# Prologue of a hybrid decoder layer on TensorE: spreading the norm row by products of high and low halves, other counts of idle turns, and the first weight's high half ahead of all token copies on ScalarE

## The chip, the cores and the metric

The kernel runs on one core of a Trainium2 chip. The metric is the device time of one execution in microseconds (us). A core has TensorE (PE; its weight loads are listed apart as PEld), VectorE (DVE), ScalarE (ACT), GpSimd (POOL) and SyncE (SP), which here only issues transfers. The engines run their own instruction lists in order and wait for each other by semaphores.

## The reference, cut to what matters

One inference step of a decoder layer with 512 prompt tokens and 32 sample tokens of width 1024. The first thing that it computes is a root-mean-square norm with a weight row `g`, and a large projection of the result; attention, a recurrent branch and a feed-forward block follow.

```python
def rmsnorm(x, g):
    x32 = x.astype(jnp.float32)
    y = x32 * lax.rsqrt(jnp.mean(x32 * x32, axis=-1, keepdims=True) + RMS_EPS)
    return (y * g.astype(jnp.float32)).astype(x.dtype)
...
    h = rmsnorm(x, g_mix_pre)
    proj = h @ w_in
```

## The kernel before

Every large product is made from high and low halves. A tile of fp32 numbers is rounded to the matmul type fp32r (the high half, a Copy on ScalarE), the rest is the fp32 number less its high half (the low half, a subtraction on VectorE or GpSimd), and TensorE adds three products: high by high, high by low, low by high. The activations `xin_hi`, `xin_lo` lie with the model dimension on the partitions, 8 tiles of 544 tokens; weights pass through a ring of two slots, `w_raw`, `w_hi`, `w_lo`.

The change touches only the prologue, that is what happens before the loop over heads. There, for five groups of tokens (four of 128, `tt` = 0 to 3, and one of 32, `tt` = TT):

- SyncE loads `x_tok` of groups 0 and 1, then weight tile 0 (`w_raw[0]`, in two transfers), groups 2 and 3, weight tile 1, and the sample tokens, in this order.
- `x_rms(tt)` on ScalarE squares and sums a group (L1684) and takes a root (L1687). `hi(0, 0, 0)` rounds weight tile 0 (L1662), and `x_hi` copies transposed tokens from PSUM to `xin_hi` (L1696), by halves of 512 columns for groups 0 to 3.
- The norm's row stands in partition 127 of `g_one`, whose other 127 partitions VectorE clears. A product with a tile of ones (`g_rows`, L1116) spreads it over 128 partitions in PSUM, and `g_copy` (L2261) on VectorE brings it to `g_row`, in two halves. `x_inv` is the reciprocal (L2266), `x_scale` the scaling of the tokens by it and by `g_row` (L2271), and `x_lo` the subtraction that leaves `xin_lo` (L2283).
- TensorE transposes scaled tokens (`x_T`, L1106), computes a small bias table (L1126, L1127), and then runs the first passes of the projection with weight tiles 0 and 1 over the columns of groups 0 and 1 (`head_pass`, L1288): three for each tile, of 8 products each. `turn(n)` is n transposes of the identity whose result nobody reads (L1113).
- GpSimd clears some tiles and makes the low half of weight tile 0 (L946) once `w_hi[0]` is there.

The order of all this is written out by hand, engine by engine. Where an instruction waits, the rest of its engine's list waits behind it. The first projection pass needs both the rounded weight and three halves of tokens, as the lines on TensorE have it:

```python
            e.wait_ge(hi_done, 1)
            e.wait_ge(xt_hi, 3)
            head_pass(0, 0, w_hi[0], xin_hi, first=True, k1=KD // 2)
            e.wait_ge(xt_hi, 4)
            head_pass(0, 0, w_hi[0], xin_hi, first=True, k0=KD // 2)
```

Of the kernel before, what the change touches and what calls it, by code (L numbers as in the profile page):

```python
# [23 lines left out]
F32 = mybir.dt.float32  # L24
F32R = mybir.dt.float32r
I32 = mybir.dt.int32
ALU = mybir.AluOpType
ACT = mybir.ActivationFunctionType
AP = bass.AP

P = 128
D = 1024
KD = D // P
# [3 lines left out]
T = SEQ + TS  # L37
# [74 lines left out]
X_ORDER = (0, 1, 2, 3, TT)  # L112
# [18 lines left out]
def program(nc, x_prompt, x_sample, cache_k, cache_v, page_table, state_conv, state_h,  # L131
# [11 lines left out]
    at = [-(-nc.sbuf_base // 64) * 64]  # L143

    def put(name, shape, dt=F32, where=None):
        size = 4 * int(np.prod(shape[1:]))
        size = -(-size // 32) * 32
        if where is None:
            offset, at[0] = at[0], at[0] + size
        else:  # L150
            offset, where[0] = where[0], where[0] + size
        assert offset + size <= nc.sbuf_usable_end, (name, offset + size)
        return nc.alloc_sbuf_tensor_at(name, shape, dt, offset=offset)
# [3 lines left out]
    w_raw, w_hi, w_lo = ring  # L157
    xin_at = at[0]
    xin_hi = put("xin_hi", [P, KD, T], F32R)
    xin_lo = put("xin_lo", [P, KD, T], F32R)  # L160
    ident = put("ident", [P, P])
    ones = put("ones", [P, P])
# [58 lines left out]
    x_sq = put("x_sq", [P, D], where=w)  # L221
    g_row = put("g_row", [P, D], where=w)
    g_one = put("g_one", [P, D], where=w)
    ssum = put("ssum", [P, 8], where=w)
    rstd_x = put("rstd_x", [P, 8], where=w)
    prow = put("prow", [56, P], where=w)
# [157 lines left out]
    with ExitStack() as ctx:  # L384
        def sem(name):
            return ctx.enter_context(nc.semaphore(name))

        ps = ctx.enter_context(nc.psum_tensor("ps", [P, 8, 512], F32))
# [12 lines left out]
        g_in = sem("g_in")  # L401
        g_spread = sem("g_spread")
# [4 lines left out]
        consts_v = sem("consts_v")  # L407
        sq_sum = sem("sq_sum")
        std_x = sem("std_x")
        norm_step = sem("norm_step")  # L410
# [661 lines left out]
        def _(e):  # L1072
# [21 lines left out]
            def x_T(tt, hfs=None):  # L1094

                rows = P if tt < TT else TS
                for hf in range(2 if tt < TT else 1) if hfs is None else hfs:
                    f = X_HALF[tt] + hf
                    e.wait_ge(xs_done, 2 * tt + hf + 1 if tt < 2 else X_ORDER.index(tt) + 3)
                    if tt == TT:  # L1100
                        e.wait_ge(sp_act, 2)
                    elif f >= 4:
                        e.wait_ge(xt_lo, f - 3)
                    kts = range(4 * hf, 4 * hf + 4) if tt < TT else range(KD)
                    for n, kt in enumerate(kts):
                        mm = e.transpose(ps[:, 4 + f % 4 if tt < TT else 3, n * rows:(n + 1) * rows],  # L1106
                                         x_tok[0:rows, tt, kt * P:kt * P + P], ident[0:rows, 0:rows])
                    mm.then_inc(xt_ready, 1)

            def turn(n):  # L1110

                for _ in range(n):
                    e.transpose(ps[:, 0, 0:P], ident[:, :], ident[:, :])  # L1113

            def g_rows(hf):
                e.matmul(ps[:, 1 + hf, :], ones[:, :], g_one[:, 512 * hf:512 * hf + 512], start=True, stop=True  # L1116
                         ).then_inc(g_spread, 1)

            turn(7)
            e.wait_ge(consts_v, 6)  # L1120
            e.wait_ge(g_in, 16)
            g_rows(0)
            g_rows(1)
            e.wait_ge(norm_step, 1)
            e.wait_ge(rel_in, 32)
            e.matmul(ps[:, 3, 0:512], rel33[:, :], bktab[:, 0:512], start=True, stop=True)  # L1126
            e.matmul(ps[:, 1, 0:RELW - 512], rel33[:, :], bktab[:, 512:RELW], start=True,  # L1127
                     stop=True).then_inc(small_T, 1)
            x_T(0, (0,))
            turn(5)  # L1130
            x_T(0, (1,))
            turn(4)
            x_T(1)
            turn(2)

# [521 lines left out]
        def _(e):  # L1657
# [18 lines left out]
            e.dma_start(rel33[0:NB, 0:HEADS], rel_bias).then_inc(rel_in, 16)  # L1676
            e.wait_ge(consts_v, 5)
            e.activation(ycol[:, 0:1], eps_col[:, :], ACT.Sqrt)

            def x_rms(tt):  # L1680

                rows = P if tt < TT else TS
                e.wait_ge(x_in[tt], 16)
                e.activation(x_sq[0:rows, :], x_tok[0:rows, tt, :], ACT.Square,  # L1684
                             accum_out=ssum[0:rows, tt:tt + 1]).then_inc(sq_sum, 1)
                e.wait_ge(sq_sum, X_ORDER.index(tt) + 1)
                e.activation(rstd_x[0:rows, tt:tt + 1], ssum[0:rows, tt:tt + 1], ACT.Sqrt,  # L1687
                             bias=eps_col[0:rows, :], scale=1.0 / D).then_inc(std_x, 1)

            def x_hi(tt, hfs=None):  # L1690

                for hf in range(2 if tt < TT else 1) if hfs is None else hfs:
                    f = X_HALF[tt] + hf
                    e.wait_ge(xt_ready, f + 1)
                    dst, src = x_fill(xin_hi, tt, hf, f)
                    e.activation(dst, src, ACT.Copy).then_inc(xt_hi, 1)  # L1696

            x_rms(0); x_rms(1)
            x_hi(0, (0,))
            hi(0, 0, 0)  # L1700
            x_hi(0, (1,))
            x_hi(1)
            x_rms(2)
            e.wait_ge(small_T, 1)
# [523 lines left out]
        def _(e):  # L2228
# [30 lines left out]
            def g_copy(hf):  # L2259
                e.wait_ge(g_spread, hf + 1)  # L2260
                e.tensor_copy(g_row[:, 512 * hf:512 * hf + 512], ps[:, 1 + hf, :]).then_inc(norm_step, 1)  # L2261

            def x_inv(tt):
                rows = slice(0, P if tt < TT else TS)
                e.wait_ge(std_x, X_ORDER.index(tt) + 1)
                e.reciprocal(rstd_x[rows, tt:tt + 1], rstd_x[rows, tt:tt + 1]).then_inc(norm_step, 1)  # L2266

            def x_scale(tt, step, c0=0, c1=D):
                rows = slice(0, P if tt < TT else TS)
                e.wait_ge(norm_step, step)  # L2270
                e.scalar_tensor_tensor(x_tok[rows, tt, c0:c1], x_tok[rows, tt, c0:c1], rstd_x[rows, tt:tt + 1],  # L2271
                                       g_row[rows, c0:c1], ALU.mult, ALU.mult).then_inc(xs_done, 1)

            def x_norm(tt):
                x_inv(tt)
                x_scale(tt, X_ORDER.index(tt) + 3)

            def x_lo(tt):
                for hf in range(2 if tt < TT else 1):
                    f = X_HALF[tt] + hf  # L2280
                    e.wait_ge(xt_hi, f + 1)
                    dst, src = x_fill(xin_lo, tt, hf, f)
                    e.tensor_tensor(dst, src, x_fill(xin_hi, tt, hf, f)[0].bitcast(F32), ALU.subtract).then_inc(xt_lo, 1)  # L2283

            g_copy(0)
            x_inv(0)
            x_scale(0, 2, 0, 512)
            g_copy(1)
            x_scale(0, 3, 512, D)
            x_inv(1)  # L2290
            x_scale(1, 4, 0, 512)
            x_scale(1, 4, 512, D)
            x_lo(0)
            x_lo(1)
            x_norm(2)
# [529 lines left out]
            op_sums(0)  # L2825
            op_low(0, 5)
            e.memset(yacc[:, :], 0.0).then_inc(consts_v, 1)
            e.wait_ge(consts_v, 7)
            y_square(0, 0)
            op_low(0, 6)  # L2830
            hs_low(2, 3)
# [75 lines left out]
```

## Time and profile before

| | |
|---|---|
| median of 3 runs | 761.62 us (760.98 to 761.72) |
| the profiled execution | 761.57 us, of which the span of its instructions is 759.7 us |
| TensorE busy | 751.6 us, 99% of the span |
| VectorE, ScalarE, GpSimd busy | 519.8, 376.5, 116.4 us |
| chain that ended last | 99% TensorE |
| TensorE's granted clock, mean | 0.997 |

The span is the time from the first to the last instruction that the profiler recorded. The busy shares are averages over the whole; the prologue is the first 20 us or so, and it has to be read by itself, in the order of time. Ends of TensorE's products are modelled, so the starts are the better measure of its pace.

### The profile page before, as it was taken

Reading aid. Unit: us, or ns where it says so; the run is one execution under the profiler, and the core shown is the slowest. Engines: PE = TensorE matmul, PEld = TensorE weight load, DVE = VectorE, ACT = ScalarE, POOL = GpSimd, SP = SyncE. Lnnn points to the kernel's source line nnn. Section 1 sums busy time; section 2 is a strip of 40 time slices with the busy share of each in tenths; the row PEclk is TensorE's granted clock in tenths of the full one; section 3 lists DMA queues with packets and bytes.
Section 4 is the critical chain, followed back from the end, with each engine's and each line's share of the span. In section 5 each row is a group of like instructions: output and inputs, shape, how many; then the busy total and the mean of one; then the engine's idle time right before and its main releaser. Section 6 shows DMA issues by size and latency. Waiting matters only on the chain.

```text
span 759.7 us, 16105 instructions
## 1 busy us (share of the span) xinstructions
PE 751.6 (99%) x5903; PEld 713.0 (94%) x5903; DVE 519.8 (68%) x823; ACT 376.5 (50%) x670; POOL 116.4 (15%) x228
## 2 busy tenths in 40 slices
PE   9999999999999999999999999999999999999996
PEld 6998899898898999997899999999999999999996
DVE  7547737656675574775469887787777899764644
ACT  7334625534733642344466555455554568454442
POOL 6502112020120110003000000000000000453650
PEclk9999999999999999999999999999999999999998
DMA  9645555545543325517461333223332212424274
GB/s 265 164 112 118 151 118 135 149 113 109 153 115 97 95 65 171 167 56 212 147 190 34 112 110 110 85 81 110 110 110 83 84 50 73 137 75 133 69 227 135
DMA packets 185065, 91.77 MB, mean 121 GB/s; under 512 B 52454, under 2 KB 177850, under 8 KB 185020
## 3 DMA queue, kind: packets, MB, share of 16 engines
q1 hardware_dynamic: 178958, 82.69, 39.8%
q0 software_dynamic: 4880, 8.13, 4.0%
q8 instruction: 28, 0.46, 0.3%
q10 hardware_dynamic: 1182, 0.35, 0.2%
q14 instruction: 17, 0.14, 0.1%
HBM read 82.37 MB, written 6.81 MB: 117 GB/s over the span
## 4 chain that ended last, share of the span: by engine, by line
PE 99%; ACT 0%; DVE 0%; DVEq 0%; issue 0%; POOL 0%; POOLq 0%
PE ps L1082 34%; PE ps L1470 28%; PE ps L1587 7%; PE ps L1365 6%; PE ps L1572 5%; PE ps L1534 4%; PE ps L1438 3%; PE ps L1288 2%; PE ps L1189 1%; PE ps L1203 1%; PE ps L1221 1%; PE ps L1263 1%; PE ps L1174 1%; PE ps L1234 1%; PE ps L1116 0%; PE ps L1373 0%
## 5 line engine op out<-in xcount | busy, mean ns | idle before, releaser
L1082 PE MATMUL ps<-xin_hi,w_hi 128*128 128x272 f32 x544 | 117.1, 296 | 0.0
L1082 PE MATMUL ps<-xin_hi,w_lo 128*128 128x272 f32 x544 | 112.6, 288 | 0.0
L1082 PE MATMUL ps<-xin_lo,w_hi 128*128 128x272 f32 x544 | 112.3, 288 | 0.0
L1082 PEld LDWEIGHTS ps<-xin_hi,w_hi 128*128 128x128 f32 x544 | 84.8, 189 | 8.1 <-issue 7.6
L2248 DVE TENSOR_TENSOR w_lo<-w_raw,w_hi 128x1024 fp32r<-128x1024 f32 (+1 forms) x46 | 55.9, 1216 | 47.6 <-ACT w_hi L1662 46.6
L1082 PEld LDWEIGHTS ps<-xin_lo,w_hi 128*128 128x128 f32 x544 | 85.5, 189 | 0.0
L1082 PEld LDWEIGHTS ps<-xin_hi,w_lo 128*128 128x128 f32 x544 | 85.0, 189 | 0.0
L648 POOL DMA_DIRECT2D ytok<-yz x48 | 33.8, 710 | 307.9 <-DVE yz L2809 307.9
L1662 ACT ACTIVATE w_hi<-w_raw 128x1024 fp32r<-128x1024 f32 (+1 forms) x47 | 49.2, 1050 | 47.9 <-PE ps L1082 44.0
L1470 PE MATMUL ps<-xq_lo,b_hi 128*128 128x272 f32 x160 | 46.7, 292 | 0.0
L1470 PE MATMUL ps<-xq_hi,a_lo 128*128 128x272 f32 x160 | 46.4, 290 | 0.0
L1470 PE MATMUL ps<-xq_lo,a_hi 128*128 128x272 f32 x160 | 46.2, 289 | 0.0
L1470 PE MATMUL ps<-xq_hi,b_hi 128*128 128x272 f32 x160 | 46.2, 289 | 0.0
L1470 PE MATMUL ps<-xq_hi,b_lo 128*128 128x272 f32 x160 | 46.1, 288 | 0.0
L1470 PE MATMUL ps<-xq_hi,a_hi 128*128 128x272 f32 x160 | 46.1, 288 | 0.0
L1470 PE MATMUL ps<-xq_hi,c_hi 128*128 128x272 f32 x160 | 46.1, 288 | 0.0
L1470 PE MATMUL ps<-xq_hi,c_lo 128*128 128x272 f32 x160 | 45.9, 287 | 0.0
L1470 PE MATMUL ps<-xq_lo,c_hi 128*128 128x272 f32 x160 | 45.9, 287 | 0.0
L1985 ACT ACTIVATE a_hi<-g_raw 128x1024 fp32r<-128x1024 f32 x20 | 21.2, 1062 | 21.1 <-PE ps L1470 17.9
L1470 PEld LDWEIGHTS ps<-xq_hi,b_hi 128*128 128x128 f32 x160 | 30.2, 189 | 0.0
L1470 PEld LDWEIGHTS ps<-xq_hi,b_lo 128*128 128x128 f32 x160 | 30.1, 188 | 0.0
L1470 PEld LDWEIGHTS ps<-xq_lo,a_hi 128*128 128x128 f32 x160 | 30.1, 188 | 0.0
(397 smaller groups left out, 2136.6 us busy)
## 6 DMA issues: line engine op xcount, KB each, us to landing
w_raw<-in_w_in_dram SPq DMA_DIRECT2D x68, 256.0 KB, 3.5
g_raw<-in_w_gate_up_dram SPq DMA_DIRECT2D x40, 256.0 KB, 3.8
u_raw<-in_w_gate_up_dram SPq DMA_DIRECT2D x20, 256.0 KB, 3.1
e_raw<-in_w_gate_up_dram SPq DMA_DIRECT2D x20, 256.0 KB, 4.3
raw_p<-in_w_down_dram SPq DMA_DIRECT2D x24, 192.0 KB, 2.5
kc<-in_cache_k_dram SPq DMA_DIRECT2D x64, 64.0 KB
vc<-in_cache_v_dram SPq DMA_DIRECT2D x64, 64.0 KB
raw<-in_w_down_dram SPq DMA_DIRECT2D x12, 320.0 KB, 3.2
```

Source lines behind the costliest of these rows:

```text
L648: e.dma_start(prompt[:, 2 * part:2 * part + 2, d, :], yz[s][rows, c0:c0 + 2 * P]).then_inc(moved, 16)
L1082: mm = e.matmul(ps[:, bank + h, 0:HT], wt[:, kw, :], xt[:, kx, h * HT:h * HT + HT], start=first and wt is wh and xt is xh, stop=last and ( ...
L1288: mm = e.matmul(ps[:, 2 * s + h, 0:cols.stop - cols.start], w[:, k, :], x[:, k, cols], start=first and k == 0, stop=last and k == KD - 1, ...
L1365: mm = e.matmul(ps[:, o_bank(tt) + c, :], xt[:, k, tt * P:tt * P + P], wt[:, c * NHALF:(c + 1) * NHALF], start=k == K_ORDER[0] and xt is x ...
L1438: mm = e.matmul(ps[:, 4 * m + 2 * c + h, 0:HT], wt[:, k, :], xt[:, x, k % KQ, :], start=k == 0 and wt is wh and xt is xq_hi, stop=k == KD ...
L1470: mm = e.matmul(ps[:, bank, 0:HT], wt[:, k0 + k, :], xt[:, x, k, :], start=first and k == 0 and wt is wh and xt is xq_hi, stop=last and k ...
L1534: mm = e.matmul(ps[:, D_BANK[odd] + h, 0:cols.stop - cols.start], wt[:, k, :], x, start=first and k == ks[0] and wt is wh and not lo_x, st ...
L1572: mm = e.matmul(ps[:, bank, 0:HT], wt[:, k, :], xt, start=first and k == 0 and wt is wh and xt is xh, stop=last and k == SK - 1 and wt is ...
L1587: mm = e.matmul(ps[:, banks[h], 0:HT], wt[:, k, :], x, start=firsts[h] and i == 0 and k == 0 and wt is wh and not lo_x, stop=lasts[h] and ...
L1662: e.activation((to or w_hi[s])[:, 0:k, :], w_raw[s][:, 0:k, :], ACT.Copy).then_inc(hi_done, count)
L1985: e.activation(a_hi[:, :, :], g_raw[s][:, :, :], ACT.Copy).then_inc(a_h, 1)
L2248: e.tensor_tensor(wl[:, 0:k, :], w_raw[s][:, 0:k, :], wh[:, 0:k, :].bitcast(F32), ALU.subtract).then_inc(lo_done, count)
```

## The change

It has three parts. The row `g` is split into a high half (`g_hi`, first 512 columns on VectorE, last 512 on ScalarE) and a low half (`g_lo`, both by VectorE), and is spread by two fp32r products per half with a tile of ones in fp32r (`ones_r`) in place of one fp32 product. On VectorE, both `g_copy` now stand ahead of the first reciprocal. The idle turns are 11, 2, 3 and 2 instead of 7, 5, 4 and 2. On ScalarE, `hi(0, 0, 0)` goes ahead of the first half of the tokens of group 0, where it stood behind it. The new tiles lie in the room of `xin_lo`, which is written later.

```diff
+    g_hi = put("g_hi", [P, D], F32R, where=w_lo_)
+    g_lo = put("g_lo", [P, D], F32R, where=w_lo_)
+    ones_r = put("ones_r", [P, P], F32R, where=w_lo_)
...
             def g_rows(hf):
-                e.matmul(ps[:, 1 + hf, :], ones[:, :], g_one[:, 512 * hf:512 * hf + 512], start=True, stop=True
-                         ).then_inc(g_spread, 1)
-
-            turn(7)
-            e.wait_ge(consts_v, 6)
-            e.wait_ge(g_in, 16)
+                half = slice(512 * hf, 512 * hf + 512)
+                e.wait_ge(norm_step, 3 + hf)
+                e.matmul(ps[:, 1 + hf, :], ones_r[:, :], g_hi[:, half], start=True, stop=False)
+                e.matmul(ps[:, 1 + hf, :], ones_r[:, :], g_lo[:, half], start=False, stop=True).then_inc(g_spread, 1)
+
+            turn(11)
             g_rows(0)
             g_rows(1)
-            e.wait_ge(norm_step, 1)
+            e.wait_ge(norm_step, 5)
...
             x_T(0, (0,))
-            turn(5)
+            turn(2)
             x_T(0, (1,))
-            turn(4)
+            turn(3)
             x_T(1)
             turn(2)
...
             e.activation(ycol[:, 0:1], eps_col[:, :], ACT.Sqrt)
+            e.wait_ge(consts_v, 6)
+            e.wait_ge(g_in, 16)
+            e.activation(g_hi[:, 512:D], g_one[:, 512:D], ACT.Copy).then_inc(consts_v, 1)
...
             x_rms(0); x_rms(1)
-            x_hi(0, (0,))
             hi(0, 0, 0)
-            x_hi(0, (1,))
+            x_hi(0)
             x_hi(1)
...
+            e.wait_ge(consts_v, 6)
+            e.tensor_copy(ones_r[:, :], ones[:, :]).then_inc(norm_step, 1)
+            e.wait_ge(g_in, 16)
+            e.tensor_copy(g_hi[:, 0:512], g_one[:, 0:512]).then_inc(norm_step, 1)
+            e.wait_ge(norm_step, 2)
+            e.tensor_tensor(g_lo[:, 0:512], g_one[:, 0:512], g_hi[:, 0:512].bitcast(F32), ALU.subtract).then_inc(norm_step, 1)
+            e.wait_ge(consts_v, 7)
+            e.tensor_tensor(g_lo[:, 512:D], g_one[:, 512:D], g_hi[:, 512:D].bitcast(F32), ALU.subtract).then_inc(norm_step, 1)
             g_copy(0)
+            g_copy(1)
             x_inv(0)
-            x_scale(0, 2, 0, 512)
-            g_copy(1)
-            x_scale(0, 3, 512, D)
+            x_scale(0, 7, 0, 512)
+            x_scale(0, 7, 512, D)
             x_inv(1)
```

On ScalarE, from the first group's squares on, the list reads so before the change (the names are those of the kernel with the buffer's number behind them; `x_sq,ssum` is a square with its sum):

```order
L1684 ACTIVATE x_sq,ssum<-x_tok 128x1024
L1687 ACTIVATE rstd_x<-ssum,eps_col 128x1
L1684 ACTIVATE x_sq,ssum<-x_tok 128x1024
L1687 ACTIVATE rstd_x<-ssum,eps_col 128x1
L1696 ACTIVATE xin_hi<-ps 128x4x128
L1662 ACTIVATE w_hi_51<-w_raw_49 128x1024
L1696 ACTIVATE xin_hi<-ps 128x4x128 x3
L1684 ACTIVATE x_sq,ssum<-x_tok 128x1024
```

and so in the changed kernel, with the copy of `g_hi` ahead:

```order
L1687 ACTIVATE g_hi<-g_one 128x512
L1693 ACTIVATE x_sq,ssum<-x_tok 128x1024
L1696 ACTIVATE rstd_x<-ssum,eps_col 128x1
L1693 ACTIVATE x_sq,ssum<-x_tok 128x1024
L1696 ACTIVATE rstd_x<-ssum,eps_col 128x1
L1668 ACTIVATE w_hi_51<-w_raw_49 128x1024
L1705 ACTIVATE xin_hi<-ps 128x4x128 x4
L1693 ACTIVATE x_sq,ssum<-x_tok 128x1024
```

One copy of tokens moved from ahead of the weight's to behind it; between the second root and the third group's squares the same five instructions stand as before.

On VectorE, from the clearing of `g_one` to the first subtraction, before:

```order
L2237 MEMSET g_one 127x1024
L2261 COPY g_row<-ps 128x512
L2266 RECIPROCAL rstd_x<-rstd_x 128x1
L2271 SCALAR_TENSOR_TENSOR x_tok<-x_tok,rstd_x,g_row 128x512
L2261 COPY g_row<-ps 128x512
L2271 SCALAR_TENSOR_TENSOR x_tok<-x_tok,rstd_x,g_row 128x512
L2266 RECIPROCAL rstd_x<-rstd_x 128x1
L2271 SCALAR_TENSOR_TENSOR x_tok<-x_tok,rstd_x,g_row 128x512 x2
```

and after:

```order
L2245 MEMSET g_one 127x1024
L2294 CAST ones_r<-ones 128x128
L2296 CAST g_hi<-g_one 128x512
L2298 TENSOR_TENSOR g_lo<-g_one,g_hi 128x512
L2300 TENSOR_TENSOR g_lo<-g_one,g_hi 128x512
L2269 COPY g_row<-ps 128x512 x2
L2274 RECIPROCAL rstd_x<-rstd_x 128x1
L2279 SCALAR_TENSOR_TENSOR x_tok<-x_tok,rstd_x,g_row 128x512 x2
L2274 RECIPROCAL rstd_x<-rstd_x 128x1
L2279 SCALAR_TENSOR_TENSOR x_tok<-x_tok,rstd_x,g_row 128x512 x2
```

Four instructions are new ahead of the first copy of the row, and the second copy moved ahead of the first group's scaling.

## Rows read from the trace of the kernel before

**Rows 1.** The page: busy time of the engines, and the last chain by engine.

```profile
PE 751.6 (99%) x5903; PEld 713.0 (94%) x5903; DVE 519.8 (68%) x823; ACT 376.5 (50%) x670; POOL 116.4 (15%) x228
...
PE 99%; ACT 0%; DVE 0%; DVEq 0%; issue 0%; POOL 0%; POOLq 0%
```

**Rows 2.** The chain that ended last, in order: start, us, what.

```profile
20.23 7.52 PE ps L1288 x56
```

**Rows 3.** Timeline, TensorE's weight loads: start, us, what, times, [idle <-releaser].

```profile
4.22 0.34 PEld L1116 LDWEIGHTS ps<-g_one,ones 128*128 128x128 f32 x1 [0.52 <-issue]
5.07 0.34 PEld L1116 LDWEIGHTS ps<-g_one,ones 128*128 128x128 f32 x1 [0.52 <-issue]
6.83 0.50 PEld L1126 LDWEIGHTS ps<-bktab,rel 128*128 128x128 f32 x2 [1.42 <-DVE rstd_x L2266]
7.82 0.19 PEld L1127 LDWEIGHTS ps<-bktab,rel 128*128 128x128 f32 x1 [0.49 <-issue]
...
16.49 1.01 PEld L1288 LDWEIGHTS ps<-xin_hi,w_hi 128*128 128x128 f32 x8 [0.23 <-ACT w_hi L1662]
...
19.55 0.57 PEld L1106 LDWEIGHTS ps<-ident,x_tok 32*128 32x128 f32 x8 [0.24 <-DVE x_tok L2271]
```

**Rows 4.** Timeline, TensorE's products in the prologue.

```profile
1.53 1.76 PE L1113 MATMUL ps<-ident 128*128 128x128 f32 x7 [1.53 <-POOL ident L928]
...
8.47 0.60 PE L1106 MATMUL ps<-ident,x_tok 128*128 128x128 f32 x4
...
10.33 1.04 PE L1106 MATMUL ps<-ident,x_tok 128*128 128x128 f32 x8
...
11.77 1.18 PE L1288 MATMUL ps<-xin_hi,w_hi 128*128 128x256 f32 x8 [0.19 <-ACT xin_hi L1696]
```

**Rows 5.** Timeline, ScalarE.

```profile
4.85 1.06 ACT L1684 ACTIVATE x_sq<-x_tok 128x1024 f32<-128x1024 f32 x1 [1.00 <-DMA x_tok<-in_x_prompt_dram]
...
7.73 0.29 ACT L1687 ACTIVATE rstd_x<-ssum,eps_col 128x1 f32<-128x1 f32 x1
9.11 0.60 ACT L1696 ACTIVATE xin_hi<-ps 128x512 fp32r<-128x512 f32 x1 [1.09 <-PE ps L1106]
9.60 1.05 ACT L1662 ACTIVATE w_hi<-w_raw 128x1024 fp32r<-128x1024 f32 x1
10.55 1.56 ACT L1696 ACTIVATE xin_hi<-ps 128x512 fp32r<-128x512 f32 x3
11.98 1.08 ACT L1684 ACTIVATE x_sq<-x_tok 128x1024 f32<-128x1024 f32 x1
```

**Rows 6.** Timeline, VectorE.

```profile
2.24 0.91 DVE L2237 MEMSET g_one<- 127x1024 f32 x1 [0.16 <-issue]
5.32 0.69 DVE L2261 COPY g_row<-ps 128x512 f32<-128x512 f32 x1 [2.17 <-PE ps L1116]
...
8.61 0.16 DVE L2266 RECIPROCAL rstd_x<-rstd_x 128x1 f32<-128x1 f32 x1
8.80 1.41 DVE L2271 SCALAR_TENSOR_TENSOR x_tok<-x_tok,rstd_x,g_row 128x512 f32<-128x512 f32 x2
10.13 0.68 DVE L2283 TENSOR_TENSOR xin_lo<-ps,xin_hi 128x512 fp32r<-128x512 f32 x1
...
13.51 0.16 DVE L2266 RECIPROCAL rstd_x<-rstd_x 128x1 f32<-128x1 f32 x1 [0.45 <-ACT rstd_x L1687]
```

**Rows 7.** Timeline, SyncE's issues of first tokens and first weight.

```profile
1.16 0.84 SPq L678 DMA_DIRECT2D x_tok<-in_x_prompt_dram  x2
...
2.53 0.51 SPq L669 DMA_DIRECT2D w_raw<-in_w_in_dram  x1
```

**Rows 8.** Transfers issued there: size, us from issue to landing.

```profile
x_tok<-in_x_prompt_dram SPq DMA_DIRECT2D x1, 512.0 KB, 3.7
...
w_raw<-in_w_in_dram SPq DMA_DIRECT2D x1, 256.0 KB, 6.4
```

More of the change, by code:

```diff
@@ L159, in program @@
     xin_hi = put("xin_hi", [P, KD, T], F32R)
+    xin_lo_at = at[0]
     xin_lo = put("xin_lo", [P, KD, T], F32R)
@@ L223, in program @@
     g_one = put("g_one", [P, D], where=w)
+    w_lo_ = [xin_lo_at]
+    g_hi = put("g_hi", [P, D], F32R, where=w_lo_)
+    g_lo = put("g_lo", [P, D], F32R, where=w_lo_)
+    ones_r = put("ones_r", [P, P], F32R, where=w_lo_)
+    assert w_lo_[0] <= xin_lo_at + 4 * KD * T
     ssum = put("ssum", [P, 8], where=w)
@@ L2275, in x_norm @@
                 x_inv(tt)
-                x_scale(tt, X_ORDER.index(tt) + 3)
+                x_scale(tt, X_ORDER.index(tt) + 7)
             def x_lo(tt):
@@ L2283, in x_lo @@
                     e.tensor_tensor(dst, src, x_fill(xin_hi, tt, hf, f)[0].bitcast(F32), ALU.subtract).then_inc(xt_lo, 1)
+            e.wait_ge(consts_v, 6)
[6 more added lines that the diff above has]
+            e.tensor_tensor(g_lo[:, 512:D], g_one[:, 512:D], g_hi[:, 512:D].bitcast(F32), ALU.subtract).then_inc(norm_step, 1)
             g_copy(0)
+            g_copy(1)
             x_inv(0)
-            x_scale(0, 2, 0, 512)
-            g_copy(1)
-            x_scale(0, 3, 512, D)
+            x_scale(0, 7, 0, 512)
+            x_scale(0, 7, 512, D)
             x_inv(1)
-            x_scale(1, 4, 0, 512)
-            x_scale(1, 4, 512, D)
+            x_scale(1, 8, 0, 512)
+            x_scale(1, 8, 512, D)
             x_lo(0)
@@ L2827, in _ @@
             e.memset(yacc[:, :], 0.0).then_inc(consts_v, 1)
-            e.wait_ge(consts_v, 7)
+            e.wait_ge(consts_v, 8)
             y_square(0, 0)
```

## The prediction

> **What bounds the kernel now.** I read the page first: TensorE is busy for 99% of the span, and the chain that ended last is TensorE for 99% [rows 1]. So the end can only move by what moves the stretch in which TensorE still waits for somebody. In the chain in order of time, TensorE runs unbroken from 20.23 us on, first 56 products in 7.52 us [rows 2]. All that the change can give or take lies before that. I therefore read the timelines of the first 20 us, engine by engine, looking at the idle time in brackets and its releaser. TensorE's first projection pass starts at 11.77 and was let go by ScalarE's copy of tokens [rows 4]; it waits for ScalarE again at 16.49 (the second weight's high half) and for VectorE at 19.55 (the sample tokens' scaling) [rows 3]. The last is the wait that fixes the end: whatever starts the passes at 11.77 earlier is worth nothing unless the token work of groups 2, 3 and TT comes earlier too. That work hangs on ScalarE, whose squares of group 2 start at 11.98, right behind the copies of groups 0 and 1 [rows 5]; VectorE waits 0.45 us for their root at 13.51 [rows 6].
>
> So the number to follow is when ScalarE gets through this block: one weight copy and four token copies. In the trace of before it starts at 9.11, when TensorE's first transposes are there, and lets the squares of group 2 start at 11.98 [rows 5].
>
> **ScalarE's new order.** ScalarE has finished the second root at 7.73 + 0.29 = 8.02 and then sits idle for 1.09 us until 9.11 [rows 5]. The change puts the weight's copy into this hole. It needs both transfers of `w_raw[0]`. The second is issued at 2.53 [rows 7] and takes 6.4 us to land [rows 8]: 8.93. That this sum is the right one is seen on the first tokens: issued at 1.16 [rows 7], 3.7 us [rows 8], 4.86, and ScalarE starts on them at 4.85 [rows 5]. So of the hole of 1.09 us only 9.11 - 8.93 = 0.18 us can be used. The weight copy then starts at 8.95, and at the spacing of before (9.60 to 10.55 for the weight, 1.56 us for three token copies, whose starts lie 0.49 apart) the token copies start at 9.90, 10.39, 10.88 and 11.37, and the squares of group 2 at 11.83 instead of 11.98 [rows 5]. Gain: 0.15 us at most, if all the transposes are there in time. The queue of SyncE isn't changed, so the landing isn't either. GpSimd's subtraction, queued behind the weight copy, starts about 0.6 us earlier. I cost that at nothing, because no row of TensorE's waits names it.
>
> **The row's new way.** Before, the first `g_copy` starts at 5.32 and VectorE ends the scaling of group 1 at 8.80 + 1.41 = 10.21 [rows 6]. After the change, from the clearing's end at 2.24 + 0.91 = 3.15:
> - `ones_r`: no row shows this cast; a quarter of the columns of the 0.68 us subtraction [rows 6] gives 0.17; with the wait ahead of it I take it to end at 3.45.
> - `g_hi`, 512 columns: between half of the 0.69 of a copy of this size from PSUM and all of it [rows 6], so 0.35 to 0.69. I take 0.6, near the copy: 4.05.
> - `g_lo`, two subtractions of 512: 0.68 each [rows 6], with a wait of 0.05 ahead of the first: 4.8 and 5.45. ScalarE's half of `g_hi` costs 0.6 (a token copy of this size [rows 5]) and lies in the 1.00 us that ScalarE waits for its first tokens before 4.85 [rows 5]. Nothing pays for it; without that cover it would be 0.6 us on all roots.
> - The products. An fp32 product of 512 columns before runs as two passes 0.85 us apart (4.22, 5.07) [rows 3], 1.7 us for a half row, at TensorE's lower clock level. An fp32r product of 512: above, one such pass, 0.85; below, the running rate at the high level, 56 products of 256 or 288 columns in 7.52 us [rows 2], which is 0.47 ns a column and 0.24 us. At the low level that doubles to 0.47, and I take 0.45. Half row 0: 4.9 to 5.8; half row 1: to 6.7 (before: 6.8).
> - `g_copy` starts 0.25 us behind the product's end (5.07 to 5.32 [rows 3, 6]): 6.05 and, waiting for the second half, 6.95 to 7.63. Then a reciprocal (0.19 from its start to the next, 8.61 to 8.80 [rows 6]), two scalings (0.70 each), a reciprocal and two scalings: 7.63 + 0.19 + 1.4 + 0.19 + 1.41 = 10.8.
>
> So the faster products do not pay for the four instructions on VectorE ahead of them: the first half row is 0.7 us later, and the chain of scalings ends about 0.6 us later than the 10.21 of before. With the low values of all the bounds it ends at 10.1, with the high ones (casts 0.1 longer, products of 0.85) at about 12.2.
>
> Is that hidden? The transposes of the first half of group 1 need its scaling at 10.1; eight transposes take 1.04 us [rows 4], four about half, so they end at 10.6, and ScalarE takes them at 10.88. Those of the second half end at 10.8 + 0.1 + 0.5 = 11.4, and ScalarE wants them at 11.37: no slack is left. VectorE's four subtractions (0.63 each) then end near 13.4 where it waits for the root of group 2 until 13.51 before [rows 6]; its idle 0.45 us hides the delay.
>
> **Idle turns.** Seven turns take 1.76 us [rows 4], 0.25 each; eleven last to 4.3, so TensorE stands idle some 0.6 us before the row's products at 4.9, where it had no gap before. The turns taken out (3 and 1) free 4 x 0.11 = 0.4 us ahead of transposes that then wait for VectorE anyway. Nothing gained.
>
> **Sum.** -0.15 us from ScalarE, +0.05 for the last transposes: -0.1 us against this execution's own 761.57 us (759.7 of span), which is 0.05 under the median of the runs. I predict 761.5.
>
> **TensorE's clock.** The granted clock reads 1.00 all through, yet the passes of an fp32 product stand 0.85 us apart at 4.22 and 5.07; and from 6.83 + about 0.15 to 7.82 the first bias product's pass takes this time too, but afterwards a pass of the same 512 columns takes half of it: the next transposes start at 8.47 [rows 3, 4]. The level went from 1.2 to 2.4 GHz near 7.8, after TensorE had been busy without a gap since 1.53.
>
> **Rivals.**
> - *The change does what it is for* (0.15): `w_raw[0]` lands earlier in the executions timed than in the one profiled, and VectorE's new casts are at their low bound. Then ScalarE's weight copy lies wholly in the hole, and the block ends behind the last transposes: scalings end at 10.1, transposes at 10.7, last copy 10.7 to 11.3 instead of 12.1. At most -0.8 us, in the middle -0.4: 761.2. Against it: the landing row.
> - *VectorE becomes the gate of the block* (0.2): casts and products at the high ends. Each 0.1 us of scaling later than 10.8 is 0.1 us later at group 2. With products at 0.6 us it is +0.5: 762.0.
> - *The clock rises late: slower* (0.12 in two cases). TensorE now has a gap of 0.6 us and shorter products in its warm-up. Before, the first product stands behind the turns at 1.53 + 1.76 = 3.3 [rows 4] and the level rises 4.5 us later; now it stands at 4.9. If the rise keeps its distance from the first product, it moves to about 9.5 (0.06): the bias products (+0.4) and four transposes (+0.4) run at the low level, and the last transposes end at 11.6: +0.1, 761.7. If it has not come by 11.8 (0.06), the 16 transposes and 7 turns up to there cost 0.11 us more each, +2.5, of which the hole before 10.9 hides about 1, and each first pass costs 0.85 more. That is +1.5 to +3: 763.1 to 764.6. It decides from a rise later than about 9.5. The Trainium skill (TensorE: Matmul & The Clock Gate, Part 4) says that transposes don't count as TensorE being busy in the way products do, which speaks for the first of the two and, with transposes alone from 8.9 to 11.8, for the second; no row here tells turns from products.
> - *Forecast* (0.5): 761.2 to 761.8, with the runs' own scatter of 0.7 us. The last 0.03 are for a cause that no row shows.
>
> **How the numbers follow.** The cases give a middle from 761.2 to 762.0 with 0.85 of the chance, and a tail upwards. The low end is the full effect less the scatter, 760.6; the high end takes in VectorE's high bounds and the late rise to 9.5 and part of its tail, 762.8. A measurement tells about 0.2%, 1.5 us. Faster than 760.1 needs more than the whole hole of 1.09 us: 0.03. Slower than 763.1 needs the clock's worse case: 0.06. The rest, 0.91, is no difference.
>
> **What the profile after would show.** Right: ScalarE's weight copy starts near 8.95, let go by the transfer and not by an engine; the four token copies follow without a gap; the squares of group 2 start at 11.8 to 12.0; the first `g_copy` is near 6.0 and the scaling of group 1 ends near 10.8; TensorE's transposes of the sample tokens start within 0.2 us of 19.55, and the rest of the kernel is as long as before. Wrong: a weight copy at 8.1 (the landing was misread); gaps between the token copies, released by TensorE (VectorE's chain is the gate); passes of the first projection spaced as at the low level (the clock); or a difference that arises behind 20 us, which no step here foresees.

## The result, and the profile after

| | before | changed |
|---|---|---|
| median, 12 runs each | 761.4 us (760.95 to 762.21) | 764.7 us (761.55 to 765.66) |
| ratio | | 1.0032, 95% interval 1.0023 to 1.0040 |
| profiled execution, span | 759.7 | 759.8 (761.59 us of device time) |

The change makes the kernel slower by 0.32%, 3.3 us of medians or 2.4 us by the ratio, which is outside the predicted range of 760.6 to 762.8. The medians hide what matters: the changed kernel's twelve times are 761.55, 761.59, 762.30, 763.38, 763.71, 764.48, and six from 764.93 to 765.66. It has executions that are as quick as before and others that cost 2 to 4 us, while these twelve times of the kernel before lie within 1.3 us. (In the later batches, two of over 1000 us aside, single executions of the kernel before reach 763.3 and, in one batch, 764.65 and 766.38.)

The profiled execution is one of the quick ones. Its rows answer to [rows 5], ScalarE:

```profile
4.71 1.06 ACT L1693 ACTIVATE x_sq<-x_tok 128x1024 f32<-128x1024 f32 x1 [0.34 <-DMA x_tok<-in_x_prompt_dram]
...
7.43 0.29 ACT L1696 ACTIVATE rstd_x<-ssum,eps_col 128x1 f32<-128x1 f32 x1
8.70 1.06 ACT L1668 ACTIVATE w_hi<-w_raw 128x1024 fp32r<-128x1024 f32 x1 [0.97 <-DMA w_raw<-in_w_in_dram]
9.66 1.23 ACT L1705 ACTIVATE xin_hi<-ps 128x512 fp32r<-128x512 f32 x2
11.06 1.09 ACT L1705 ACTIVATE xin_hi<-ps 128x512 fp32r<-128x512 f32 x2 [0.17 <-PE ps L1112]
12.03 1.06 ACT L1693 ACTIVATE x_sq<-x_tok 128x1024 f32<-128x1024 f32 x1
```

and to [rows 3, 4, 6], VectorE and TensorE, with GpSimd's subtraction for the first weight:

```profile
5.94 0.69 DVE L2269 COPY g_row<-ps 128x512 f32<-128x512 f32 x1 [0.71 <-PE ps L1125]
9.11 0.75 DVE L2279 SCALAR_TENSOR_TENSOR x_tok<-x_tok,rstd_x,g_row 128x512 f32<-128x512 f32 x1
9.78 0.75 DVE L2279 SCALAR_TENSOR_TENSOR x_tok<-x_tok,rstd_x,g_row 128x512 f32<-128x512 f32 x1
...
9.84 2.95 POOL L952 TENSOR_TENSOR w_lo<-w_raw,w_hi 128x1024 fp32r<-128x1024 f32 x1 [1.14 <-ACT w_hi L1668]
...
11.80 1.19 PE L1294 MATMUL ps<-xin_hi,w_hi 128*128 128x256 f32 x8
19.59 0.68 PE L1112 MATMUL ps<-ident,x_tok 32*128 32x32 f32 x8
```

In this execution all is close to the forecast: the weight's copy waits for the transfer, the squares of group 2 start at 12.03 (before 11.98 [rows 5]), and the sample transposes at 19.59 (before 19.55 [rows 3]). But one row is odd. GpSimd's subtraction takes 2.95 us, and it starts 0.06 us after VectorE's last scaling of group 1. These rows of the profile of before answer to it and to a second pair that comes up further down, all from the timeline:

```profile
9.47 0.74 DVE L2271 SCALAR_TENSOR_TENSOR x_tok<-x_tok,rstd_x,g_row 128x512 f32<-128x512 f32 x1
11.17 1.89 DVE L2283 TENSOR_TENSOR xin_lo<-ps,xin_hi 128x512 fp32r<-128x512 f32 x3 [0.35 <-ACT xin_hi L1696]
25.93 0.17 DVE L2334 TENSOR_SCALAR prm<-sp 128x4 f32<-128x4 f32 x1
...
10.74 2.39 POOL L946 TENSOR_TENSOR w_lo<-w_raw,w_hi 128x1024 fp32r<-128x1024 f32 x1 [2.15 <-ACT w_hi L1662]
26.02 3.54 POOL L960 COPY bias_s<-bias_rev 128x256 f32<-128x256 f32 x4 [3.00 <-DMA bias_rev<-dist_shift]
```

There the subtraction took 2.39 us, and it started at 10.74, when the scaling had ended at 10.21. The second pair has such a sign too: of the four copies into `bias_s` three took about 0.66 us there and one 1.72, which is why the row says 3.54 where a trace further down has 2.48.

Two more executions of the changed kernel took 765.01 and 765.29 us. The trace of the first, the same engines:

```profile
8.64 1.06 ACT L1668 ACTIVATE w_hi<-w_raw 128x1024 fp32r<-128x1024 f32 x1 [0.74 <-DMA w_raw<-in_w_in_dram]
...
9.79 2.35 POOL L952 TENSOR_TENSOR w_lo<-w_raw,w_hi 128x1024 fp32r<-128x1024 f32 x1 [1.09 <-ACT w_hi L1668]
...
9.78 2.91 DVE L2279 SCALAR_TENSOR_TENSOR x_tok<-x_tok,rstd_x,g_row 128x512 f32<-128x512 f32 x1
...
12.74 0.66 PE L1112 MATMUL ps<-ident,x_tok 128*128 128x128 f32 x4 [2.17 <-DVE x_tok L2279]
...
21.47 0.68 PE L1112 MATMUL ps<-ident,x_tok 32*128 32x32 f32 x8
...
26.01 2.48 POOL L966 COPY bias_s<-bias_rev 128x256 f32<-128x256 f32 x4 [3.07 <-DMA bias_rev<-dist_shift]
...
25.77 3.56 DVE L2346 SCALAR_TENSOR_TENSOR sp<-sp,sp 128x4 f32<-128x4 f32 x9
...
30.99 0.52 PE L1088 MATMUL ps<-xin_hi,w_hi 128*128 128x272 f32 x2 [1.31 <-DVE w_lo L2263]
```

Here are two losses, each an overlap of VectorE with GpSimd. **The first collision**: GpSimd's subtraction now takes its usual 2.35 us and it is VectorE's scaling that takes 2.91 instead of 0.75. TensorE stands idle for 2.17 us, and the sample transposes come at 21.47 instead of 19.59, 1.88 later. **The second collision**: VectorE's series of nine tiny instructions for the recurrent branch's parameters (`sp`, 128x4) meets GpSimd's four copies into `bias_s` and takes 3.56 us. In the quick execution the same nine have this row, and the copies there start behind them, at 26.10:

```profile
23.89 1.74 DVE L2346 SCALAR_TENSOR_TENSOR sp<-sp,sp 128x4 f32<-128x4 f32 x9
```

Behind the series in VectorE's list stands the low half of the next weight, and TensorE waits 1.31 us for it at 30.99. The two make 1.88 + 1.31 = 3.2 us of the 3.42 by which this execution is longer than the quick one. The second of these traces has the same two losses: the subtraction starts at 9.61, 0.17 us ahead of the scaling, the scaling takes 2.85 us, TensorE is idle for 1.43 us, the sample transposes come at 21.41, the series of nine takes 3.46 us, and TensorE waits 1.24 us ahead of 30.87.

### The profile page after: what moved, and what is told of

Same layout as the page of the kernel before. It is cut to its first block, busy times and chain, and to the rows that moved or that the text cites. A ratio compares the mean times of both kernels' runs of the same rounds, so it can differ in the third digit from the quotient of the medians.

```text
span 759.8 us, 16110 instructions
## 1 busy us (share of the span) xinstructions
PE 751.1 (99%) x5903; PEld 713.7 (94%) x5903; DVE 521.1 (69%) x827; ACT 377.1 (50%) x671; POOL 116.9 (15%) x228
## 4 chain that ended last, share of the span: by engine, by line
PE 97%; DVE 1%; ACT 1%; issue 0%; DVEq 0%
PE ps L1088 34%; PE ps L1476 28%; PE ps L1593 7%; PE ps L1371 6%; PE ps L1578 5%; PE ps L1540 4%; PE ps L1444 3%; PE ps L1195 1%; PE ps L1209 1%; PE ps L1227 1%; PE ps L1294 1%; PE ps L1269 1%; PE ps L1180 1%; PE ps L1240 1%; PE ps L1379 0%; PE ps L1406 0%
```

## The experiments

Theory 1 (later B) was TensorE's clock: it rises late in some executions, because the change leaves a gap and shorter products in its warm-up. Theory 2 was the weight's transfer, with the token copies queued behind it. Theory A, that GpSimd and VectorE hold each other up, came from the trace of `after_gap_closed`; A2 is the same theory with both places of collision. The runs were made in four batches, each on another chip and with its own runs of the kernel before, whose medians were 761.5, 761.4, 761.62 and 761.28; so runs of different batches are best compared by their ratios to before.

**The parts alone.** ScalarE's order alone (`order_only`):

```diff
             x_rms(0); x_rms(1)
-            x_hi(0, (0,))
             hi(0, 0, 0)
-            x_hi(0, (1,))
+            x_hi(0)
             x_hi(1)
```

> The kernel before with ScalarE's new order alone (the first weight's high half ahead of the first token copy). Theory 1, the clock: the changed kernel's executions lie in two heaps, near 761.6 and near 765, because TensorE rises from 1.2 to 2.4 GHz late in some of them, and that comes from what TensorE does in its first 9 us. Here TensorE's first 9 us are as before, so all executions lie within 761.0 to 762.2, 0.0 to 0.2 us under before. Theory 2, the transfer: ScalarE waits for the weight's landing with the token copies queued behind it, and in most executions the weight lands some 3 us later than in the profiled one. Then this kernel shows the heap near 765 too.

Measured: 761.66 us (760.98 to 764.06), ratio 1.0005 (0.9996 to 1.0014). There is no heap near 765, so theory 2 falls; the traces of 765 us say the same directly, for the weight's copy starts at 8.64 and 8.47 in them and at 8.70 in the quick one. The one time at 764.06 fits neither expectation.

The turns alone (`turns_only`: `turn(7)`, `turn(5)`, `turn(4)` to 11, 2, 3).

> The kernel before with the new counts of idle turns alone (11, 2, 3, 2 for 7, 5, 4, 2). Theory 1a, turns keep the clock's warm-up alive between the transposes: with 6 of them gone behind the row's products the late rise comes here too, a heap near 765. Theory 1b, what counts is the real products and the gap ahead of them: the row's fp32 products still follow the turns without a gap, only 1.0 us later, and the transposes after them are unchanged, so 761.4 to 762.4, the row being 1.0 us later of which the hole of 1.09 us on ScalarE hides most.

Measured: 761.67 us (760.82 to 763.30), ratio 1.0003 (0.9994 to 1.0012): 1b, not 1a. Its profiled execution (762.99 us) has the second collision by itself, without the first: no long scaling, but `bias_s` copies from 24.42 on, in the middle of the parameters, and this wait of TensorE's weight loads:

```profile
28.44 0.30 PEld L1082 LDWEIGHTS ps<-xin_hi,w_hi 128*128 128x128 f32 x2 [1.28 <-DVE w_lo L2255]
```

The row's new way alone (`row_only`: the changed kernel with ScalarE's order and the turns put back).

> The changed kernel with the old turns (7, 5, 4, 2) and ScalarE's old order, so that only the row's spread by high and low halves is left of the change; TensorE then has a gap of some 1.4 us ahead of the row's products. Theory 1 (the clock, from the gap and the shorter products): two heaps, some executions near 765, the median at or above that of the changed kernel. Theory 2 (the transfer ahead of the token copies on ScalarE): no heap near 765, since the weight's copy is behind the first token copy again; about 761.6 to 762.2.

Measured: 763.19 us (761.84 to 764.42), ratio 1.0022 (1.0014 to 1.0031). The row is the part that costs, even with the old order. Seven of its 12 executions lie from 763.07 to 764.42, the others from 761.84 to 762.13. Its trace is one of the quick ones (762.07), and in it the first collision is far off: GpSimd's subtraction, behind the weight's copy of the old order, starts at 11.28, and the scaling has ended at 10.53. The second pair all but meets: VectorE's parameters end at 26.61, and the copies start at 26.57. That points to the second collision for the slower seven; no trace of one was taken.

**The gap closed** (`after_gap_closed`: `turn(11)` to `turn(14)` in the changed kernel).

> The changed kernel with 14 turns instead of 11 ahead of the row's products, which closes the gap of 0.54 us there with transposes of the identity. If the gap makes the clock rise late, the heap near 765 is gone and all executions lie near 761.6 to 762.0. If turns don't count for the clock, or the shortness of the row's products is the cause, the heaps stay, median 763 to 765.

Measured: 763.01 us in the median of twelve, 760.92 to 763.09 in seven runs and 765.74 to 766.87 in four (one more took 1414 us); ratio 1.0018 (1.0000 to 1.0035). The heaps stay, so the gap is not the cause. Its profiled execution took 766.82 us and showed the first collision unasked, a scaling of 2.84 us, and a third thing. The table by stretches of TensorE's granted clock (columns: stretch, length, busy time and instructions of PE, PEld, DVE, ACT and POOL, granted clock, DMA share, GB/s):

```profile
6.00:13.00 7.00, 4.61 (x27) 2.91 (x27) 6.84 (x9) 4.07 (x7) 5.06 (x9) 1.00 1.09 330
13.00:14.00 1.00, 1.00 (x9) 1.00 (x8) 1.00 (x3) 0.70 (x2) 0.00 (x0) 0.65 1.19 236
14.00:20.00 6.00, 6.00 (x29) 5.61 (x29) 5.37 (x10) 5.48 (x12) 2.50 (x5) 0.50 0.85 208
21.00:25.00 4.00, 4.00 (x39) 3.83 (x37) 3.06 (x6) 2.35 (x6) 1.61 (x4) 1.00 0.67 194
```

The level was 2.4 GHz, fell to 1.2 near 13.3, after TensorE had stood idle for 2.10 us behind the long scaling, and came back near 20. So the clock can add to the collision, but in this trace as its follower. In the 765 us traces of the changed kernel itself it did not fall, though one of them has 2.17 us of idle time at the same place. The mean granted clock of each execution tells such falls apart: it is 0.993 in all four of the upper heap here, and 0.996 to 0.998 in all twelve executions of the changed kernel. The kernel before has the low mean as well, in two executions of the second batch (764.65 at 0.995, 766.38 at 0.994). This mean does not show when the level first rises, since the granted clock reads 1.00 before that too.

**A guard on the first collision** (`after_pool_waits`, the changed kernel):

```diff
             e.wait_ge(hi_done, 1)
+            e.wait_ge(xs_done, 4)
             e.tensor_tensor(w_lo[0][:, :, :], w_raw[0][:, :, :], w_hi[0][:, :, :].bitcast(F32), ALU.subtract
```

> The changed kernel in which GpSimd's subtraction for the first weight's low half also waits for the fourth scaling on VectorE. Theory A, the collision: one execution's trace showed VectorE's last scaling of group 1 taking 2.84 us instead of 0.75 while GpSimd's subtraction (9.67, 2.35 us) ran, and TensorE idle for 2.1 us behind it; whichever of the two starts first holds the other up, and the change brought their starts within 0.1 us of each other. With the wait GpSimd is always second: no scaling over 0.8 us, the heap at 765 is gone, all executions within 761.0 to 762.5. Theory B, the clock alone (thinner work of TensorE in its warm-up): nothing on TensorE differs from the changed kernel, the heap at 765 stays and the median is 763 to 765.

Measured: 763.94 us (761.63 to 767.17), ratio 1.0026 (1.0011 to 1.0042). A miss for theory A as it stood. Only one of 11 executions is above 764.9 now (767.17, with a mean granted clock of 0.994), where the changed kernel had six of 12, but a new heap of seven stands at 763.3 to 764.3. Something was left, and the traces of the next two showed what. The one trace of this kernel is of a quick execution (761.63), so the heap itself was not seen at work.

> The kernel before with ScalarE's new order alone, and the same wait on GpSimd. Theory A: the scalings end at about 10.0 here and GpSimd would start at 9.9, so a few executions without the wait collided (its slowest was 764.06); with it the spread is that of the kernel before, 760.8 to 762.5, and the median 0.0 to 0.3 us under before. Theory B has no reason for a difference to the run without the wait, 761.66.

Measured (`order_pool_waits`): 761.96 us (760.86 to 765.10), ratio 0.9998 (0.9984 to 1.0012), inconclusive for the first collision. Its profiled execution (765.10 us) is of use: the tokens and the weight landed late there (ScalarE's weight copy starts at 10.05), TensorE stood idle 1.41 us, its granted clock was 0.57 from 14.5 to 18, and VectorE's series of nine took 3.51 us beside GpSimd's copies, the second collision again. Here the lateness came from the transfers, without the first collision.

**The first collision forced** (`collision_forced`):

```diff
             x_scale(1, 8, 0, 512)
+            e.wait_ge(hi_done, 1)
+            e.memset(junk[:, :], 0.0)
             x_scale(1, 8, 512, D)
```

> The changed kernel in which VectorE waits for the first weight's high half and clears a scratch tile of 256 columns ahead of the last scaling of group 1, so that GpSimd's subtraction always starts first. The clearing itself costs at most 0.3 us. Theory A: every execution has a last scaling of 2.3 us or more and lies at 764 or above, up to 767; the trace shows TensorE's granted clock falling to 1.2 GHz behind the idle stretch in the dearer ones. Theory B: +0.3 us on the changed kernel, with two heaps as there.

Measured: 765.01 us (762.38 to 765.93), ratio 1.0038 (1.0024 to 1.0052); 9 of 11 executions are above 764. Theory A expected all of them there; the other two, 762.38 and 762.91, lie even below what the forced collision costs alone (763.54 and more, below), and nothing on record explains them. The profiled one has a scaling of 2.58 us, and a series of nine of 3.14 us with a wait of TensorE of 1.24 us at 30.86. The clock did not fall, in this execution or by its mean in any of the eleven (0.996 to 0.998).

> The same forced collision, with 20 turns of the identity on TensorE between the transposes of the two halves of group 1, which fill the 2.1 us in which it stood idle. If idle time there is what lets the clock fall, the clock stays at 2.4 GHz and only the collision's own 1.8 to 2.4 us are left: 763.4 to 764.0 in all executions. If transposes of the identity don't hold the clock up, it costs as much as without them, 764 to 767.

Measured (`collision_turns`): 766.45 us (765.93 to 767.15), 5 runs, ratio 1.0060 (1.0036 to 1.0084). A miss. The trace shows why the test says nothing of the clock: the 20 turns last from 11.29 to 13.47 and hold up the transposes, which in the forced collision started at 12.70. The 20 turns were longer than the hole, which was 1.22 us in the forced collision, and the second collision came too. Besides, the clock had not fallen in the forced collision, so there was no fall for the turns to prevent.

**A guard on the second collision**, in four kernels:

```diff
             e.wait_ge(bias_moved, 16 * (DEC_T + 1 + PAIRS))
+            e.wait_ge(small_c, 4)
             for f in range(PAIRS):
                 src = bias_rev[:, f, DEC_T:DEC_T + PAST][:, ::-1].rearrange("p (n i a) -> p n a i", n=NPG, i=BLK)
```

> The forced collision of before, and GpSimd's copies into bias_s held back until VectorE has finished the parameters (semaphore small_c at 4). The forced collision's trace showed two losses: its scaling (2.58 us for 0.75) moved all work behind it by 1.85 us, and then VectorE's chain of small parameter instructions met GpSimd's four copies into bias_s, each small instruction taking up to 0.6 us instead of 0.17, so that TensorE waited 1.24 us at 30.86 for a weight's low half. Theory A2, both are the same lock between VectorE and GpSimd: with the copies held back the second loss is gone and the time falls by 1.3 to 1.7 us, to 763.3 to 763.7 in nearly all executions. Theory B, the loss at 31 us comes from a late transfer or the clock: no change, 765.0.

Measured: 763.67 us (763.54 to 764.73, 6 runs), ratio 1.0029 (1.0017 to 1.0041), where the forced collision without the guard had 765.01. Behind a first collision the second is worth 1.3 us (1.6 against each batch's own runs of before), and the first, which alone is left here, with the clearing of at most 0.3 us that forces it, lies 2.0 us above before. Its trace: the scaling takes 2.58 us, GpSimd's copies wait for VectorE, the series of nine is back at 1.74 us.

```profile
10.06 2.58 DVE L2281 SCALAR_TENSOR_TENSOR x_tok<-x_tok,rstd_x,g_row 128x512 f32<-128x512 f32 x1
25.75 1.74 DVE L2350 SCALAR_TENSOR_TENSOR sp<-sp,sp 128x4 f32<-128x4 f32 x9
...
28.04 3.32 POOL L968 COPY bias_s<-bias_rev 128x256 f32<-128x256 f32 x4 [5.17 <-DVE prm L2354]
```

> The changed kernel with the same guard on the copies into bias_s alone. Theory A2: the heap at 765 moves to 763.2 to 763.8 (the first collision stays, the second cannot happen); the fast executions stay at 761.6; median 763.4. Theory B: as the changed kernel, 764.7.

Measured: 763.04 us (761.30 to 763.75), ratio 1.0015 (1.0006 to 1.0023). The heap at 765 is gone, five of 11 lie at 763.38 to 763.75, as expected. The trace is of a quick execution (761.46): the subtraction starts at 10.16, the scaling has been running since 9.78 and keeps its 0.74 us, and the subtraction takes 2.62.

> The changed kernel with both guards, GpSimd's subtraction behind the last scaling of group 1 and its copies into bias_s behind the parameters. Theory A2: no collision is left, 761.4 to 762.3 in nearly all executions. If a heap at 763 or above stays, a third cause is at work, the late rise of TensorE's clock being the first candidate, since its rise lies at 8.6 to 9.6 us in the traces of kernels with the new row and at 6.4 to 7.8 in those without it.

Measured: 761.93 us (761.27 to 763.87), ratio 1.0006 (0.9998 to 1.0015). With both guards 2.8 us of the changed kernel's 764.7 are back; two of 12 executions are still above 763, and no trace of such a one was taken. The expectation's times for the rise of the level don't cover all traces without the new row: in that of `turns_only` the row's fp32 passes stand 0.43 us apart from 4.61 on, so it was up by then, 0.7 us after the first product and with turns alone ahead of it.

> The kernel before with the guard on the copies into bias_s alone. In its trace the parameters end at 26.0 and the copies start at 26.02, so a little lateness of VectorE or a little earliness of GpSimd's transfers makes them meet. Theory A2: the median stays within 0.2 us of before and the executions above 762 become fewer. If GpSimd's work is late for something else, a new wait appears and the time rises by 0.3 us or more.

Measured: 761.20 us (760.95 to 761.88), ratio 0.9994 (0.9986 to 1.0003). No time above 762, where the kernel before had 9 of 30 in the same batch. By chance alone this would come out in about one case of 25, so it suggests, and does not show, that the kernel before pays for the second collision now and then; no trace of such an execution was taken. What `turns_only` shows is that the second collision needs neither the new row nor the new order. This is the version with the lowest median; it is 0.4 us below before, which its interval doesn't tell from nothing.

**What is left.**

> The changed kernel as it is, to have the trace of another of its executions. Nine of its twelve times were above 763. If this one is, theory A2 expects in its trace a scaling of group 1 of 2.3 us or more against 0.75, a wait of TensorE of 1 to 2 us ahead of the last transposes of group 1, and, when the time is 764.5 or above, small parameter instructions of up to 0.6 us between 24 and 30 us and a wait of TensorE near 31 us. A clock that rises late without them would speak for theory B. If its time is below 762.5 neither is there.

> The changed kernel once more, for the trace of one more execution, with the same expectation: both collisions in it at 764.5 or above, the first alone at 763 to 764, none below 762.5.

Measured: 765.01 and 765.29 us, and in both traces the two collisions, as shown above. Theory A2 holds for ordinary executions; theory B falls for them: the level was up before 9.7 us in both and stayed. By the spacing of the products it rose near 7.9 and 9.3 in these two and near 8.9 in the quick one, so the time does not follow it.

> Only the row's new way (old turns, ScalarE's old order), with both guards on GpSimd. Without them it was 763.19. Its scalings end 0.3 us later than in the kernel before and ScalarE's weight copy, behind the first token copy, starts 0.55 us later (9.6 to 10.15). Theory A2: no collision, so no execution near 764; what is left is that lateness of the block on ScalarE, 761.9 to 762.3, which is the row's own price of some 0.5 us.

Measured: 762.04 us (761.80 to 762.99), ratio 1.0012 (1.0003 to 1.0021): the row's own price, 0.8 us by medians and 0.9 by the ratio, without any execution near 764. The trace shows 0.33 us of it, in ScalarE's block as expected: the first projection pass starts at 12.10 instead of 11.77 [rows 4], and the sample transposes at 19.88 instead of 19.55 [rows 3].

```profile
9.43 0.60 ACT L1707 ACTIVATE xin_hi<-ps 128x512 fp32r<-128x512 f32 x1 [1.84 <-PE ps L1114]
9.93 1.05 ACT L1670 ACTIVATE w_hi<-w_raw 128x1024 fp32r<-128x1024 f32 x1
...
12.10 1.18 PE L1296 MATMUL ps<-xin_hi,w_hi 128*128 128x256 f32 x8 [0.19 <-ACT xin_hi L1707]
```

> The kernel before with ScalarE's new order and both guards on GpSimd. Theory A2: all executions within 760.7 to 762.2, median 0.2 to 0.5 us under the kernel before: the order's gain, which is the part of ScalarE's hole ahead of the transposes that the weight's landing leaves.

Measured: 761.40 us (761.02 to 763.24), ratio 1.0004 (0.9995 to 1.0013). No gain from the order, where 0.2 to 0.5 us was expected, and one execution above 763 in spite of both guards. In its trace the squares of group 2 start at 11.65 and the sample transposes at 19.20, 0.35 earlier than in the profile of before, but the kernel before itself varies by as much: in `before_bias_late`, with the old order, they start at 19.16.

## Why the prediction was wrong

**The step that failed** is in the part on ScalarE's new order: "GpSimd's subtraction, queued behind the weight copy, starts about 0.6 us earlier. I cost that at nothing, because no row of TensorE's waits names it." The subtraction did start earlier, at 9.6 to 9.8 (before 10.74), and no row of TensorE's waits named it. But it ran into VectorE's last scaling, which the row's new way had moved from 9.47 to 9.78. One moved by some 1.0 us and the other by 0.3 us, towards each other, and where 0.5 us had lain between the scaling's end and the subtraction's start, the two now start within 0.2 us. The prediction's own figures had them meet: its last scaling runs from 10.1 to 10.8, and 0.6 us ahead of 10.74 is 10.1. Whichever is first holds up the other: 0.06 us ahead, VectorE lost nothing and GpSimd took 0.56 us longer; 0.17 us behind (the trace of 765.29 us), VectorE lost 2.1 us. In the trace of 765.01 us, where it lost 2.2, the recorded starts are 9.78 and 9.79, too close to tell who was first. That is why the changed kernel has heaps, and why the one profiled looked harmless. Forcing the order gave the upper heap (765.01, in 9 of 11 executions), guarding both places took it away (761.93). Neither the order alone nor the turns alone cost anything that could be measured; of the parts alone only the row did (1.0022), and with both guards it is 1.0012. The rest of the sum held within the noise: with both guards the whole change is at 1.0006 (0.9998 to 1.0015), and the forecast of -0.1 us is 0.9999.

The Trainium skill (SBUF — State Buffer, "Who interferes with whom") says that a VectorE instruction with two SBUF inputs contends with a GpSimd instruction that reads SBUF, and that whoever issues first has the shared ports for the whole instruction while the other blocks. The traces agree: the scaling (two tensors in SBUF) took 2.91 us beside a subtraction of 2.35 that began with it. They agree in the negative too: the subtractions into `xin_lo`, with one input in PSUM, kept 0.63 us each beside GpSimd's subtraction, which lay over them from 10.74 to 13.13 in the trace of before (1.89 us for three, from 11.17). Read against the order of the two lists, this rule would have made the collision a rival.

**The second collision was missed too.** A delay of 1.9 us at 13 us was not the end: "TensorE runs unbroken from 20.23 us on" was read as if nothing behind that point could change. In the profile of before VectorE's parameters end at 26.1 and GpSimd's copies start at 26.02, a cover of nothing. VectorE's work shifted by 1.9 us and GpSimd's, which hangs on transfers, did not: 26.01 in the trace of 765 us. So 1.3 us more were lost at 31 us, which is the prediction's own last sign of being wrong, a difference behind 20 us. The second collision is not only a follower of the first: with the first guarded (`after_pool_waits`) the ratio was still 1.0026, and with both guarded it was 1.0006. Either collision alone put the median outside the range, 763.04 with the second guarded and 763.94 with the first.

**What held.** The landing of the first weight gates ScalarE (8.70 against 8.95 forecast; the transfer took 6.1 us instead of 6.4). The first `g_copy` came at 5.94 (6.05), the scaling of group 1 ended at 10.53 (10.8), its transposes were the last gate of ScalarE's block (0.17 us of idle time, released by TensorE), and no gain came of the hole. With both guards the changed kernel takes 761.93, 0.1 beyond the forecast's own 761.2 to 761.8, and inside the range. The rival "the clock rises late" named a time near the measured one, 763.1 to 764.6, but its mechanism isn't in the two traces of 765 us, and none of the changed kernel's twelve executions has the low mean of a fallen clock. The level did fall in two other kernels' traces, in both after idle time of over a microsecond ahead of the first pass. One sum was off without effect: with the high values of its bounds the prediction's chain of scalings ends near 12.5, not 12.2.

**What stays open**: which of the two made the four executions of the changed kernel between 762.3 and 764.48 and the heaps of `row_only` and `after_pool_waits`, of which no slow execution was traced; the two executions above 763 with both guards; why seven of 11 executions of `after_pool_waits` are that slow, when in its one trace VectorE is not late; and whether turns of the identity keep the clock up, since the one test of that had no fall to prevent. The trace of `turns_only`, where the level rose with little but turns ahead of it, speaks for turns counting, but it is one trace.

## What to carry to other kernels

When an edit moves an instruction of GpSimd or VectorE, look for what the other engine does at its new time, not only for who waits for its result: two instructions without any dependence can hold each other up, here for nearly the length of the other one (2.1 to 2.2 us of a subtraction of 2.35 to 2.47), and a race of hundredths of a microsecond then decides from run to run. A row that got longer without a reason (2.95 for 2.39 us) is how the harmless side of such a race showed in a profile here, and heaps in the list of times are how it showed in the result; take a trace of an execution from the upper heap before explaining the median. And where "unbroken from here on" rests on two engines passing within a tenth of a microsecond, it is not a bound: a delay ahead of it can be paid twice.

## What the runs showed of the hardware

- Even instructions of four elements a partition are held up: the nine of the series took 0.16 us each alone and up to 0.58 beside GpSimd's copies, which take 0.65 to 0.69 each.

```profile
L2346 DVE SCALAR_TENSOR_TENSOR sp<-sp,sp x9: 161/240/582, 25.8 to 29.1; 128x4 f32<-128x4 f32 x9
```

- The cast of 512 columns to fp32r on VectorE took 0.42 us and that of 128 columns 0.23; an fp32r product of 512 columns at TensorE's lower level took 0.43 from start to start, half of a pass of an fp32 product (0.85).
- The granted clock fell to 0.50, that is 1.2 GHz, in the middle of the prologue after TensorE had idled 2.1 us, and the passes of 8 products of 256 columns then took 2.0 us instead of 1.2 (`after_gap_closed`). In `again_a` it stayed at 1.00 after 2.17 us of idle time at the same place, so the idle time alone did not decide it.
